# A three-layer hybrid model on one core: parameters packed beside the constants, the first loads reordered, and the router's tables made later

## The reference

```python
def hierarchical_moe(h, w_r1, b_r1, w_r2, b_r2, w1, w3, w2):
    grp_logits = t @ w_r1 + b_r1                       # 4 groups
    grp_gate = softmax(grp_logits)[argmax]
    fine_sel = (t @ w_r2 + b_r2)[chosen group]         # 8 experts in it
    top_val, top_idx = lax.top_k(fine_sel, 2)
    gate = grp_gate * softmax(top_val)
    ...
    def expert_block(xb, e):
        a = silu(xb @ w1[e]) * (xb @ w3[e])
        return a @ w2[e]
    y[token] += gate * expert_block(...)
```

## Time and profile before

| | |
|---|---|
| median of 3 runs | 1824.82 us (1824.7 to 1825.04) |
| the profiled execution, its own time | 1826.98 us |
| its span | 1825.2 us |
| TensorE busy | 1563.2 us, 86% |
| VectorE, ScalarE busy | 402.8 us (22%), 293.3 us (16%) |
| moved by DMA | 380.81 MB |
| mean granted clock of TensorE | 0.937 |

### The profile page before, as it was taken

One profiled execution on the slowest core, in us unless ns is written; L12 is line 12 of the kernel. 1 busy time (PEld: TensorE's weight loads), 2 busy tenths in 40 slices (PEclk: granted clock), 3 DMA queues, 4 the chain that ended last, 5 costly groups with the idle time before them and its releaser, 6 DMA issues.

```text
span 1825.2 us, 17152 instructions
## 1 busy us (share of the span) xinstructions
PE 1563.2 (86%) x7214; PEld 982.2 (54%) x7214; DVE 402.8 (22%) x967; ACT 293.3 (16%) x599; POOL 75.6 (4%) x115
## 2 busy tenths in 40 slices
PE   5999989999999999989999999998966665665555
PEld 2577878588644678878588544445542221222121
DVE  0227642211000226632111001346240000000001
ACT  1224322011000214332111001115210000000000
POOL 4000000000000000000000003000000000000000
PEclk9999999999999999999999999999968887778888
DMA  9345322444443543213334436640639999999998
GB/s 266 126 164 198 112 93 93 147 151 163 138 151 109 171 141 139 71 69 139 138 140 170 152 138 185 224 150 1 264 140 409 409 409 409 410 409 409 409 409 324
DMA packets 142575, 380.81 MB, mean 209 GB/s; under 512 B 6629, under 2 KB 16901, under 8 KB 142305
## 3 DMA queue, kind: packets, MB, share of 16 engines
q1 hardware_dynamic: 113056, 268.53, 40.4%
q0 software_dynamic: 29440, 111.15, 15.9%
HBM read 378.03 MB, written 5.73 MB: 210 GB/s over the span
## 4 chain that ended last, share of the span: by engine, by line
PE 71%; DMA 23%; DVE 3%; issue 2%; ACT 1%; SPq 0%; POOL 0%; DVEq 0%; ACTq 0%; POOLq 0%
PE bank L834 27%; DMA region<-in_w 20%; PE bank L841 18%; PE bank L1080 12%; DMA ring<-in_w 2%; PE bank L1175 2%; PE bank L1013 2%; DMA ring<-in_w_in 1%; PE bank L1042 1%; PE bank L1044 1%; PE bank L897 1%; PE bank L1193 1%; PE bank L873 1%; PE bank L1048 1%; PE bank L885 1%
## 5 line engine op out<-in xcount | busy, mean ns | idle before, releaser
L834 PE MATMUL bank<-hT,ring 128*128 128x256 f32 x2240 | 496.9, 382 | 11.5 <-ACT region L1416 7.2
L834 PEld LDWEIGHTS bank<-hT,ring 128*128 128x128 f32 x2240 | 425.6, 192 | 75.6 <-issue 18.1
L841 PE MATMUL bank<-ring,region 128*128 128x512 f32 (+3 forms) x608 | 214.4, 513 | 17.2 <-DMA ring<-in_w_in 8.6
L1080 PE MATMUL bank<-ring,region 128*128 128x512 f32 x512 | 220.4, 592 | 0.0
L841 PEld LDWEIGHTS bank<-ring,region 128*128 128x128 f32 x608 | 111.8, 194 | 114.1 <-issue 90.4
L1080 PEld LDWEIGHTS bank<-ring,region 128*128 128x128 f32 x512 | 97.1, 190 | 120.6 <-issue 120.3
L1175 PE MATMUL bank<-ring,region 128*32 128x512 f32 x512 | 78.0, 748 | 64.0 <-DMA ring<-in_w 63.0
L1175 PE MATMUL bank<-region 128*32 128x512 f32 x512 | 78.0, 748 | 59.1 <-DMA region<-in_w 59.1
L841 PE MATMUL bank<-ring,hT 128*128 128x512 f32 x256 | 110.6, 592 | 1.8 <-DVE hT L1530 1.8
L1175 PEld LDWEIGHTS bank<-ring,region 128*32 128x32 f32 x512 | 17.8, 131 | 118.7 <-DMA ring<-in_w 75.7
L841 PEld LDWEIGHTS bank<-ring,hT 128*128 128x128 f32 x256 | 48.3, 190 | 61.9 <-issue 61.9
(11 more groups left out here) (319 smaller groups left out, 1307.1 us busy)
## 6 DMA issues: line engine op xcount, KB each, us to landing
ring<-in_w_in SPq DMA_DIRECT2D x28, 2048.0 KB, 7.8
ring<-in_w SPq DMA_DIRECT2D x24, 2048.0 KB, 35.9
region<-in_w SPq DMA_DIRECT2D x24, 2048.0 KB, 36.0
ring<-in_w POOLq DMA_DIRECT2D x24, 2048.0 KB, 37.2
region<-in_w POOLq DMA_DIRECT2D x24, 2048.0 KB, 37.2
ring<-in_w_up SPq DMA_DIRECT2D x16, 2048.0 KB, 7.6
ring<-in_w_down SPq DMA_DIRECT2D x16, 2048.0 KB, 7.8
ring<-in_w_out SPq DMA_DIRECT2D x6, 2048.0 KB, 8.0
```

Of the source, the lines that this page charges most:

```text
L834: t = mm(b[:, 0:T], w[:, k, :], act[:, k, :], start=(k == 0), stop=(k == KD - 1))
L841: t = mm(b[:, 0:cols], act(k)[:, i * P:(i + 1) * P], w[:, k, :], start=(k == 0), stop=(k == KD - 1))
L1080: t = mm(b[:, :], hid[:, 8 * kb + k, i * P:(i + 1) * P], w[:, k, :], start=(kb == 0 and k == 0), stop=(kb == 3 and k == KD - 1))
```

## The change

1. **Constants and parameters in one array.** `par` and its tile are gone. The host lays the parameters out (`host_parameters`) behind the identity at the head of the constants. A first DMA loads the 144 columns with the identity and `g_mix` (576 B per partition, 74 KB), then come `x`, chunk zero and chunk one, and then the other 4120 columns (2.1 MB). GpSimd issues the three bias tables only.
2. **The norm before the router.** ScalarE squares `x` in halves as they arrive; the first half of the router's products stands ahead of the turning of the second half of `x`; VectorE makes `xn3` directly behind the reciprocal, before it reads the router's logits.
3. **Tables behind the first products.** `pick` is made in two parts, experts 0 to 7 first, ahead of the dense gate; `gather(0)` follows the ranks; `gateT` and `put` are turned between the two first groups of expert products (`turn_tables`), in banks 4 to 7, and copied behind the first expert operation of each engine. `put0` lies in `hT`, so that it no longer shares its place with `xg` and `yslot`.

SyncE's and GpSimd's queues:

```diff
+            sp.dma_start(cst[:, 0:FIRST], a["c_main"][:, 0:FIRST]).then_inc(first_loaded, 16)
             sp.dma_start(x[:, :, :], a["x"].rearrange("b (i p) d -> p (b i) d", p=P)).then_inc(x_loaded, 16)
-            sp.dma_start(cst[:, :], a["c_main"]).then_inc(consts_loaded, 16)
             for n, (_, l, name, r0, kt, c0, w) in enumerate(chunks):
                 if n == 2:
+                    sp.dma_start(cst[:, FIRST:], a["c_main"][:, FIRST:]).then_inc(consts_loaded, 16)
                     sp.dma_start(mem_rows, a["mem_2"].rearrange("b (i p) d -> p (b i) d", p=P)).then_inc(mem_loaded, 16)
...
-            pool.dma_start(g_mix[:, 0, :], a["norm_mix"][0].rearrange("(k p) -> p k", p=P)).then_inc(gain0_loaded, 16)
             pool.dma_start(t5_onehot, a["c_t5"]).then_inc(t5_loaded, 16)
             pool.dma_start(t5_rows, a["c_t5m"]).then_inc(t5_loaded, 16)
             pool.dma_start(t5_tab, a["t5_table_2"]).then_inc(t5_loaded, 16)
-            for l in range(DEPTH):
...
```

TensorE:

```diff
-            pe.wait_ge(consts_loaded, 16)
+            pe.wait_ge(first_loaded, 16)
...
                     if name == "hi":
 
+                        pe.wait_ge(consts_loaded, 16)
                         pe.wait_ge(diag_ready, l + 1)
...
+            turned(N_FFN, 0)
+            for i in range(NT):
+                token_major((2, "router", i), wr, h_tile, i, (0,))
             turn_half(N_FFN, 1)
-            turned(N_FFN, 0)
             turned(N_FFN, 1)
             for i in range(NT):
-                token_major((2, "router", i), wr, h_tile, i)
+                token_major((2, "router", i), wr, h_tile, i, (1,))
...
+            def turn_tables():
+
+
+                pe.wait_ge(gates_made, 1)
+                b = bank_of((2, "gateT"))
+                for i in range(NT):
+                    t = turn(b[0:N_EXP, i * P:(i + 1) * P], fine[2][:, i, :], ident)
+                full(t, (2, "gateT"))
+                pe.wait_ge(put0_ready, 1)
...
             def gather(q):
+                pe.wait_ge(pick_ready, 1 if q < 2 else 2)
...
-            wait_freed([(2, "put", j) for j in range(4)])
             gather(0)
...
                     full(t, (2, "up", q, j))
+                    if q == 0 and j == 0:
+                        turn_tables()
```

ScalarE (after it, the copies of `put` 0 and 2 stand behind the first sigmoid of quad 0):

```diff
-            norm(N_FFN)
...
+            for half in range(2):
+                for i in range(NT):
+                    if half and i:
+                        ffn_rows(0)
+                    act.wait_ge(*there[half][i])
+                    cs = slice(512 * half, 512 * half + 512)
+                    A_(xn3[:, i, cs], src[:, i, cs], ACT.Square, accum_out=ss_ffn[:, i, half:half + 1]
+                       ).then_inc(ffn_squared, 1)
+            ffn_rows(2)
+            act.wait_ge(ffn_summed, 1)
+            A_(sd[:, N_FFN, :], ss[:, N_FFN, :], ACT.Sqrt, bias=eps_c, scale=1.0 / D).then_inc(ss_ready, 1)
```

VectorE (the two operations of `put0` stand unchanged between `rows_of_quad(0)` and the loop over the quads):

```diff
-            norm(N_FFN)
-            dve.wait_ge(rs_ready, N_FFN + 1)
...
+            ffn_rows(3)
+            dve.wait_ge(ffn_squared, 2 * NT)
+            V.tensor_reduce(ss[:, N_FFN, :], ss_ffn, AX.X, ALU.add).then_inc(ffn_summed, 1)
+            dve.wait_ge(ss_ready, N_FFN + 1)
+            link(V.reciprocal(rs[:, N_FFN, :], sd[:, N_FFN, :]))
+            dve.wait_ge(gain_row_loaded, 16)
+            for i in range(NT):
+                V.scalar_tensor_tensor(out=xn3[:, i, :], in0=x[:, i, :], scalar=rs[:, N_FFN, i:i + 1], in1=gain_row,
+                                       op0=ALU.mult, op1=ALU.mult).then_inc(h_rows_ready, 1)
...
+            for e0, e1 in ((0, 8), (8, N_EXP)):
+                for i in range(NT):
+                    t = V.tensor_tensor(pick[:, i, e0:e1], bc(slot_no.unsqueeze(1), [e1 - e0, CAP]),
+                                        bc(fine[0][:, i, e0:e1].unsqueeze(2), [e1 - e0, CAP]), ALU.is_equal)
+                t.then_inc(pick_ready, 1)
...
+            rows_of_quad(0)
+            dve.wait_ge(pick_ready, 2)
...
                 own(key)
+                if q == 0:
+                    t = V.tensor_copy(gateT[0:N_EXP, :], read((2, "gateT"))[0:N_EXP, 0:T])
+                    free(t, (2, "gateT"))
+                    own((2, "gateT"))
+                    V.tensor_copy(gateT[N_EXP:N_EXP + 1, 0:8], gateT[0:1, 0:8]).then_inc(gateT_ready, 1)
+                    for j in range(1, 4, 2):
...
```

More of the change, by code:

```diff
@@ L263, in build @@
         rs_idx = s_(DEPTH, NT)
+        ss_ffn = s_(NT, 2)
         lb, omlb = s_(DEPTH, N_HG), s_(DEPTH, N_HG)
@@ L576, in build @@
             used((2, ("wo", n)), (2, "wo", n, 1))
-        give_turns(2, "h2T", 1)
         for i in range(NT):
             bk.give((2, "router", i))
+        give_turns(2, "h2T", 1)
         bk.give((2, "rank"))
-        bk.give((2, "gateT"))
+        bk.give_at((2, "gateT"), 7)
         for j in range(4):
-            bk.give((2, "put", j))
+            bk.give_at((2, "put", j), 4 + j)
         for r in range(4):
@@ L1148, in _ @@
             xn3_rows = xn3.rearrange("p i (c m k) -> p i c k m", c=4, k=2)
+            def turn_tables():
[5 more added lines that the diff above has]
+                pe.wait_ge(put0_ready, 1)
+                rows = put0.rearrange("p i e s -> p i (e s)")
+                for j in range(4):
+                    b = bank_of((2, "put", j))
+                    for h in range(2):
+                        for i in range(NT):
+                            t = turn(b[:, T * h + P * i:T * h + P * i + P],
+                                     rows[:, i, P * (2 * j + h):P * (2 * j + h) + P], ident)
+                    full(t, (2, "put", j))
             def gather(q):
+                pe.wait_ge(pick_ready, 1 if q < 2 else 2)
                 for n in range(2):
@@ L1198, in _ @@
                         t.then_inc(expert_chunk_used, 1)
+                if q == 0:
+                    wait_freed([(2, "put", j) for j in range(4)])
                 for n in range(2):
@@ L1460, in _ @@
             A_(one[4], one[4], ACT.Exp).then_inc(router_exps, 1)
-            for j in range(0, 4, 2):
-                key = (2, "put", j)
-                free(A_(put[:, 2 * j:2 * j + 2, :], read(key)[:, :].rearrange("p (e t) -> p e t", e=2), ACT.Copy), key)
             def rows_of_quad(q):
@@ L1471, in _ @@
                 A_(quad_hid, read((2, "up", q, 0))[:, :], ACT.Sigmoid).then_inc(experts_up, 1)
+                if q == 0:
+                    for j in range(0, 4, 2):
+                        key = (2, "put", j)
+                        free(A_(put[:, 2 * j:2 * j + 2, :], read(key)[:, :].rearrange("p (e t) -> p e t", e=2), ACT.Copy),
+                             key)
                 if q + 1 < QUADS:
@@ L1932, in _ @@
             rows_of_quad(0)
+            dve.wait_ge(pick_ready, 2)
+            for i in range(NT):
+                t = V.tensor_tensor(put0[:, i], pick[:, i], bc(fine[5][:, i, :].unsqueeze(2), [N_EXP, CAP]), ALU.mult)
+            t.then_inc(put0_ready, 1)
             for q in range(QUADS):
```

139 lines of the change are left out of this document (56 added, 83 removed).

## The result

The changed kernel takes 1803.94 us (median of 4 runs, 1802.77 to 1806.35) against 1824.93 us before (median of 4): ratio 0.9887, 95% interval 0.9875 to 0.9899. The forecast was 1803.2 us in a range of 1799.8 to 1807.5. Two later sets gave the changed kernel 1807.92 and 1807.71 us, just outside that range, beside a kernel before that was 1.1 and 1.6 us slower as well. The profiled execution took 1803.26 us, its span is 1801.4.

The account below looks back on a forecast made before the run. TensorE was taken to bound the kernel up to about 1292 us, weight transfer the experts. Start 10.8 plus experts 10.8 (1.4 + 11.0 - 1.6) is 21.6 us off 1824.82: 1803.2 us, range 1799.8 to 1807.5.

Parts of the forecast that it names:

- What bounds, and where the gain comes from: TensorE bounds up to about 1292 us, weight transfer the experts; time is lost at the kernel's start and the experts' start.
- signs of being wrong: Chunk zero past 14 us, queue gap between chunks 10 and 9, stream under 405 GB/s, or `hi` projection waiting for constants.
- signs of being right: Included: first matmul on chunk zero at 12 to 13 us, queues idle 19 us and not 30, 409 GB/s behind it.
- The start: First weight chunk at the kernel's start: lands at 12.4 us and not 23.2, gain 10.8 us, between 7.3 and 11.6.
- Rival (a): At the start, GpSimd's tables still hold chunk zero to 248 GB/s: gain 7.3 us and not 10.8, 1806.7 us; chance 0.08.
- The moved constants: At the start, 2.11 MB of constants behind chunk one cost nothing; without cover the price would be 5.8 us.
- Norm and router: Ahead of the experts, the router's chain starts sooner: gain 1.4 us, ends 0.7 and 3.
- Tables: Between router's chain and `gather(0)`: 12.0 us shrink to 1.0, two operations of 256 columns and hand-overs; gain 11.0 us.
- Clock: At gather and chunk 0, TensorE runs longer at half clock: cost 1.6 us, between a gain of 2.1 and loss of 2.4.
- What the moved tables cost behind: Behind the first expert products: transposes and copies hidden; chunk 9 has some 2 us of cover, up to 2 us lost.
- Rival (d): In the expert stream, SyncE's and GpSimd's queues stay out of step at 362 GB/s: 59 us more, 1862 us; chance 0.01.
- The sum: Whole kernel: 10.8 us at the start plus 10.8 at the experts, 21.6 us less, median 1803.2 us; chance 0.68.

Follow-up runs that it names:

- The start alone: The kernel before with only the two queues' first loads, the waits that go with them and the constants' new layout changed: 1816.36 us, ratio 0.9943.
- the order alone: The kernel before with the identity first and the other constants behind chunk one, parameters still GpSimd's small loads: 1818.92 us, one run.
- sets 1 and 3: Two of three later sets run beside the kernel before on one chip; the changed kernel took 1807.92 us in set 1 and 1807.71 us in set 3.

## Why the prediction was right, and where its terms were not

**What bounds, and where the gain comes from: right.** Both places on the chain moved as said, and of the signs of being wrong none came in the first profile: chunk zero at 13.8 us (13.7 to 14.04 over all profiles of this start) against a limit of 14, no gap between chunks 9 and 10, a stream of 409 GB/s. Of the signs of being right two came short: chunk zero was not at 12 to 13 us, and the queues idled some 16.5 us (1317 to 1333.5) and not 19. Run alone the two parts give 9.7 and 7.6 us by the medians of one set, the whole change 18.1 in it and 21.0 in the first comparison, for the forecast 21.6.

**The start: 10.8 forecast, 9.4 measured.** The term that was mis-sized is the landing of `x`: the tables' 0.22 MB were put beside chunk zero and not beside `x`, which landed 1.9 us later than said (8.4 and not 6.5), because GpSimd's tables, whose packets came behind `x` before, now come beside it. The 5.4 us from `x` to chunk zero are less than the 5.9 that were allowed. Rival (a) named these tables as what could slow the start, with a price of 3.5 us; they cost 1.65. The 436 GB/s of the Trainium skill's fit for GpSimd's path (DMA: Bandwidth & Descriptors, section "Anatomy of one DMA — SWDGE (gpsimd) path") are not reached by this load on SyncE's queue: 2.10 MB in 5.4 us are 388 GB/s. The prediction put the slow stretch down to the columns of 4-byte elements; shown is that the order carries 4.5 us of the gain and all the small loads together 4.9. The moved constants cost nothing, as argued.

**Norm and router: 1.4 forecast, 1.7 measured** (from the experts' load to the router's chain 38.45 us before, 36.73 after). The root was done at 1310.98, 4.7 us behind the end of the last output product (4.9 in the forecast), and the last router product ended before the logits were read. One sum of the prediction is off without harm: half of 6.07 us, halved again, is 1.5 and not 1.8; the row took 1.87.

**Tables: 11.0 forecast, 11.1 measured** (12.15 to 1.06 us). The row of 2.50 us merges two operations of 256 columns and two of 768; only the first two stand ahead of the gather, which begins 0.86 us behind their start, for the 0.8 and a hand-over of 0.1 that were put.

**Clock: a loss of 1.6 forecast; against the profile before a gain of 0.2, against the old order at full clock a loss of 2.0.** The gather took 5.97 us; the granted clock came back at about 1328 us, 4.4 us into it, and chunk 0 was multiplied at full clock in 1.8 us. The step that was wrong is the starting point: the prediction took the 6.17 us of the one profile before as what the gather costs behind the turning of `put`. The start alone and the order alone have the same turning ahead of it, and there it took 4.01 us. That fits the forecast's cause, that without the turning the gather runs at half clock for longer, and its size nearly: the third number is 10.4 us less than in those two, for the forecast 10.8. The cause was not run by itself, and it rests on three profiles of the old order, of which two have the gather at full clock, and ten of the new, of which none has. The 13.0 of the first pair hold 2.6 us of a slow draw in the profile before. The 6.8 us of a gather wholly at half clock was too low as well: twice the 4.04 us at full clock are 8.1.

**What the moved tables cost behind: 0 to 2 us forecast, some 3 to 4 measured, and in another way.** (470.3 to 471.2 us at the end for the changed kernel, 466.9 to 468.1 in the kernels with chunk 9 in time.) The prediction looked at GpSimd's queue, and at whether the queues would run dry between chunks 10 and 9. They did not: 391 GB/s and more in every stretch of 2 us from 1338 to 1380, and 409 from there to 1780. But the lag stays. Each queue issues its next chunk when its own slot comes free, so nothing lets GpSimd's catch up; the stream goes on at 409 GB/s, and the bill comes after 450 us: GpSimd's chunk 91 lands only some 11 us ahead of the stream's end and not 15.6, and TensorE, which may go on only behind it, is what is late. The queues fall silent at about 1788 us and TensorE is through with chunk 95 at 1792.9, 5 us later; before these were about 1815.5 and 1817.4, 2 us. That SyncE's queue stays ahead through all eight quads is shown by the medians from issue to landing, 27.2 against 37.0 us. Rival (d) had the queues out of step, and priced it as a loss of rate, of which there is none.

**The sum: in part luck.** The 23.8 us between the two profiles are 9.4 + 5.1 + 13.0 - 3.7. Of these, 5.1 are the luck of the second cut and 2.6 that of the third. Without the second the terms give 18.7 us; without both, and against the ends of the two kernels with the old tables (467.75 and 468.09), they give 9.4 + 10.4 - 3.0 = 16.8. The medians of sets 1 and 3 give 18.1 and 18.8, those of the first comparison 21.0. So the forecast's 21.6 is some 3 us above those two medians and 4.8 above the terms, by the 1.4 of the start, 0.4 in the experts' start and the 3.0 at the end of the stream, which was put at nothing in the sum; that it met the first median within 0.7 us is luck of the draw.

## What to carry to other kernels

Where transfers feed the end of a kernel, find the moment at which the stream is asked to restart, and take everything off the path to it; but follow each queue's first issue behind that moment too, since a lag between two queues that share a stream lasts to the end and is paid there, where no dip in bandwidth shows it. At a kernel's start many small loads, or a table on a second queue, can cost more than their bytes: 29 loads with 0.6 MB took 4.9 us here, in which one load moves 1.9 MB at 388 GB/s. Before the sum of terms is held against one profile, cut both profiles at common events: a stretch that the change doesn't touch shows how much of the difference is luck. And read a term's starting value from more than one profile: the 2.6 us in the experts' start showed only in the kernels that had kept it.

## What the runs showed of the hardware

One program's stretch of 1264 us took between 1263.6 and 1268.4 us in three executions of the same kernel, for the larger part by a half-clock stretch of TensorE behind a wait of 3.3 us (a product of 17.04 us in place of 13.97); which of the waits is followed by one differs from execution to execution. The Trainium skill (TensorE: Matmul & The Clock Gate, section "What's actually happening") has the clock follow the engine's recent activity as seen by a free-running monitor, and the trace agrees that the same sequence falls on either side.

Three tables of 0.22 MB on GpSimd's queue, in rows of 6 KB on few partitions, delayed a load on SyncE's queue by 1.7 us: 333 to 358 GB/s between 3 and 13 us with them, 383 without.

Two queues that share a stream, each waiting for its own slots, kept a lag of 6 us for 450 us at an unchanged 409 GB/s: the leading queue's loads landed 27.2 us behind their issue and the other's 37.0, against 36.8 and 37.2 without the lag.
